# Summing the squares of the second norm: three more tiles on GpSimd, and one sum on TensorE behind the second projection

## The chip, the cores and the metric

The kernel runs on one core of one Trainium2 chip. The metric is the device time of one execution in microseconds (us), the median over several runs.

## What is computed

Two batches of 512 tokens with 1024 features go through two layers with shared weights: a pooling mixer and a SwiGLU feed-forward, then grouped-query attention (8 query heads, 2 key/value heads, head size 128, axial rotary positions) and a second SwiGLU. An RMS norm stands ahead of each of the four. The part that the change touches is the norm ahead of attention, and the projections that follow it:

```python
def rms_norm(x, g):
    xf = x.astype(jnp.float32)
    y = xf * lax.rsqrt(jnp.mean(xf * xf, axis=-1, keepdims=True) + EPS)
    return (y * g.astype(jnp.float32)).astype(x.dtype)

h = rms_norm(x, norm_mix[1])
qkv = jnp.einsum('btd,de->bte', h, w_qkv)
q, k = rms_norm(q, q_gain), rms_norm(k, k_gain)
q, k = apply_axial_rope(q, tables), apply_axial_rope(k, tables)
x = x + attention(q, k, v) @ w_o
```

## The kernel before

Each engine has its own written-out list of instructions, and semaphores tie the lists together; every engine and every DMA queue takes its list in order. The residual stream `x` lies in SBUF with features on partitions, as 8 tiles of 128 features by 512 tokens for each batch, so that a sum over features is a sum over partitions and tiles. Products with weights are made in three float32r matmuls each (high·high, high·low, low·high).

Norm k (1 to 3 in the code) works on 16 tiles in the order `SEQ[k]`; its position in that order is called `r`. ScalarE squares each tile (`square`, L1103). A squared tile goes one of two ways:

- GpSimd adds it to a running sum `stat[b]` of its batch (`add_squares`, L2422). At the end TensorE sums that one tile over partitions (`mean_square`), with four matmuls against a column of ones, one for each 128 tokens.
- Tiles in the list `DIRECT[k]` are summed by TensorE themselves (`sum_square`), four such matmuls for each tile, into the same PSUM columns.

A plain float32 matmul leaves two records in the trace, so one `mean_square` or one `sum_square` is 8 records of line L596. Then ScalarE takes the root (`root`, L1111), VectorE the reciprocal (`inverse`, L1691), TensorE spreads the result over partitions (`wide`, four transposes, L603), and ScalarE keeps it (`keep_wide`, L1117).

For norm 2, the first 12 tiles of `SEQ[2]` go through GpSimd: batch 0 wholly, and half of batch 1. The last four tiles (features 4 to 7 of batch 1) are final only when the last block of the first feed-forward, block 41, has been added to `x` (`add_rows(0, 6)`). They are in `DIRECT[2]`, and their squares lie in the four tiles `late[3:7]`. Batch 1's `mean_square(2, 1)` is placed between blocks 39 and 40 of the feed-forward's second matmul (L784).

The stretch after the feed-forward, in the order of each list:

- TensorE: `project(0)` (the first key head of batch 0, 24 matmuls, L583), `project(1)` up to feature tile 3, with `head_square(0)` (8 records, L899) after tile 1, four `sum_square` for r = 12 to 15, the rest of `project(1)` (12 matmuls), `key_wide(0)`, `wide(2, 1)`, then `values(0, ...)` in four quarters (24 matmuls each, L924) with `head_square(1)` after the first, `key_wide(1)` after the second, then `project(2)` and on. The third quarter needs weight unit 3, `key_wide(1)` needs `head_inverse(1)`.
- ScalarE: the squares r = 12 to 15, `gain(0)` (a square L1486 and a scaled copy L1487; it writes the tiles that GpSimd's running sum also reads, `tmp[4]` and `tmp[5]`, and so waits for `n_acc`), `head_root(0)`, `split(2)`, `root(2, 1)`, `gain(1)`, `keep_wide(2, 1)`, `split(3)`, `key_hi(0)`, `head_root(1)`.
- VectorE: `split_lo(1)`, `split_lo(2)`, `head_inverse(0)`, `inverse(2, 1)`, `rope(0)`, `split_lo(3)`, `key_lo(0)`, `head_inverse(1)`, `rope(1)`. `split_lo(i)` (L1684) ends the preparation of weight unit i. `rope(p)` is three instructions, L2198, L2202 and, for keys, L2206, and it waits for the rotated copy from DMA, for both rotary tables, and for GpSimd's `times_cos(p)` (L2462).
- The SP queue, which issues the DMAs: weight unit 4 (`load_att(4)`), the cosine table (L513), the sine table (L515), weight unit 5 (L383), four DMAs of 64 KB for `rotate(0)` (L503), four for `rotate(1)`, weight unit 6, and on.

The sine table is loaded into `tmp[7]`, which is also `stat[1]`, the running sum of batch 1. Its load therefore waits until `mean_square(2, 1)` has read that tile:

```python
sp.wait_ge(n_ms, 2)
sp.dma_start(sin_t[:, :], rope_sin).then_inc(tables_in, 16)
```

Of the kernel before, what the change touches and what calls it, by code (L numbers as in the profile page):

```python
# [13 lines left out]
KC = D // P  # L14
# [42 lines left out]
NBLK = (NPAIR + 1) // 2  # L57
N_BLOCK = 7 * NBLK
# [3 lines left out]
def build(nc, x_prompt, x_sample, norm_mix, norm_ffn, pool_w, pool_b, pool_scale, w_qkv, q_gain,  # L62
          k_gain, w_o, w_gu, w_down, rope_cos, rope_sin, band_tab, y_prompt, y_sample):
    with ExitStack() as ctx:
# [96 lines left out]
        b_gate, b_up, b_down = bank[0:2], bank[2:4], bank[4:8]  # L161
# [6 lines left out]
        def sem(name):  # L168
            return ctx.enter_context(nc.semaphore(name))
# [14 lines left out]
        n_sq, n_acc, n_add, n_ms, n_sqrt = sem("n_sq"), sem("n_acc"), sem("n_add"), sem("n_ms"), sem("n_sqrt")  # L184
# [52 lines left out]
        def q_of(h, b):  # L237
# [8 lines left out]
        SEQ = {1: [(c, b) for b in range(NB) for c in range(KC)],  # L246
               2: ([(c, 0) for c in range(4, 8)] + [(c, 1) for c in range(4)] + [(c, 0) for c in range(4)]
                   + [(c, 1) for c in range(4, 8)])}
# [2 lines left out]
        GAIN = {1: V_FFN, 2: V_MIX + KC, 3: V_FFN + KC}  # L251


        DIRECT = {1: SEQ[1], 2: SEQ[2][12:], 3: SEQ[3][15:]}
        ACC0, ADD0 = {1: 0, 2: 0, 3: 10}, {1: 0, 2: 16, 3: 20}

        def acc_count(k, r):

            return ACC0[k] + sum(1 for cb in SEQ[k][:r + 1] if cb[0] != HEAD[k][cb[1]] and cb not in DIRECT[k])

        def add_count(k, r):

            return ADD0[k] + sum(1 for cb in SEQ[k][:r + 1] if cb in DIRECT[k])

# [3 lines left out]
        def last_of(k, b):  # L268
            return max(i for i, cb in enumerate(SEQ[k]) if cb[1] == b and cb not in DIRECT[k])

# [88 lines left out]
        def _(sp):  # L359
# [139 lines left out]
            def rotate(p):  # L499

                sp.wait_ge(p_gain, p + 1)
                for dst, src in ((0, 1), (1, 0), (2, 3), (3, 2)):
                    sp.dma_start(rot[p % 2][32 * dst:32 * dst + 32, :],  # L503
                                 qg[p % 2][32 * src:32 * src + 32, :]).then_inc(rot_in[p % 2], 16)
# [3 lines left out]
            for i in range(NB * N_QKV):  # L508
                load_att(i + RAW)
                b, j = i // N_QKV, i % N_QKV  # L510
                if i == 1:
                    sp.wait_ge(n_lo, KC)
                    sp.dma_start(cos_t[:, :], rope_cos).then_inc(tables_in, 16)  # L513
                    sp.wait_ge(n_ms, 2)
                    sp.dma_start(sin_t[:, :], rope_sin).then_inc(tables_in, 16)  # L515
                elif i == 2:
                    for p in range(KVH):
                        rotate(p)
                elif b == 1 and j < 2:
                    rotate(N_PROJ * b + j)  # L520
                elif j >= 4:
                    rotate(N_PROJ * b + j - 2)
# [55 lines left out]
        def _(pe):  # L578
# [8 lines left out]
            def three(whi, wlo, mhi, mlo):  # L587
                return [(whi, mhi), (whi, mlo), (wlo, mhi)]
# [27 lines left out]
            def mean_square(k, b, out):  # L616

                pe.wait_ge(n_acc, acc_count(k, last_of(k, b)))
                return columns(stat[b], out, True)
# [189 lines left out]
            def swiglu(layer):  # L809
                k = 2 * layer + 1  # L810
                gate_up(layer, 0, 1)
                if layer == 0:
                    sum_square(1, 14, bank[3])
                else:
                    mean_square(3, 1, bank[3])
                sum_square(k, 15, bank[3])
                gate_up(layer, 0, 2)
                wide(k, 1, bank[5])
                gate_up(layer, 1, 1)
                gate_up(layer, 1, 2)  # L820
                gate_up(layer, 0, 5)
                gate_up(layer, 2, 1)
                gate_up(layer, 1, 5)
                gate_up(layer, 2, 2)
                gate_up(layer, 0, 6)
                gate_up(layer, 0, 3)
                gate_up(layer, 1, 6)
                gate_up(layer, 0, 7)
                gate_up(layer, 1, 3)
                gate_up(layer, 0, 4)  # L830
                gate_up(layer, 1, 7)
                gate_up(layer, 1, 4)
                gate_up(layer, 2, 6)
                gate_up(layer, 2, 5)
                gate_up(layer, 2, 7)
                gate_up(layer, 2, 3)
                gate_up(layer, 2, 4)
                for i in range(3, NF):
                    gate_up(layer, i, 1)
                    gate_up(layer, i, 5)  # L840
                    gate_up(layer, i, 6)
                    gate_up(layer, i, 3)
                    gate_up(layer, i, 7)
                    gate_up(layer, i, 2)
                    gate_up(layer, i, 4)
                for b in range(N_BLOCK):
                    if layer == 0 and b == N_BLOCK - NBLK + 2:
                        mean_square(2, 0, bank[1]).then_inc(n_ms, 1)
                    elif layer == 0 and b == N_BLOCK - NBLK + 3:
                        wide(2, 0, bank[1])  # L850
                    elif layer == 0 and b == N_BLOCK - NBLK + 4:
                        mean_square(2, 1, b_up[1]).then_inc(n_ms, 1)
                    if layer == 1 and N_BLOCK - NBLK < b < N_BLOCK - NBLK + 4:
                        u = 4 * (b - (N_BLOCK - NBLK + 1))
                        for i in range(u, u + 4):
                            turn_y(i)
                    down_block(layer, b)
# [4 lines left out]
            def project(p, out, bank_free, ks=range(KC)):  # L862

                b, u = p // N_PROJ, unit_of("p", p)
                if 0 in ks:
                    if bank_free > 0:
                        pe.wait_ge(p_gain, bank_free)
                    if p == N_PROJ:
                        pe.wait_ge(n_lo, 2 * KC)
                    elif p == N_PLAIN - 1:  # L870
                        pe.wait_ge(v_lo_done, 2)
                    elif p == N_PLAIN:
                        pe.wait_ge(v_lo_done, 4)
                    pe.wait_ge(w_lo, u + 1)
                for k in ks:
                    whi, wlo = w_chunk(u, k)
                    if p == 0:
                        pe.wait_ge(n_lo, k + 1)
                    product(out[:, :], three(whi, wlo, half_hi[b][:, k, :], half_lo[b][:, k, :]),
                            k == 0, k == KC - 1, proj_done if k == KC - 1 else None)  # L880
                    if k == 1 and p > 0 and p not in (KVH, N_PLAIN):
                        if p <= N_PLAIN:
                            head_square(p - 1, b_up[(p - 1) % 2], p - 2)
                        else:
                            head_square(p - 1, b_side[1][:, NT * (p - 1 - N_PLAIN):], N_PLAIN + 4 if p == N_PLAIN + 5 else 0)
# [44 lines left out]

            project(0, b_gate[0], 0)
            project(1, b_gate[1], 0, range(4))
            for r in range(12, 16):
                sum_square(2, r, b_up[1])
            project(1, b_gate[1], 0, range(4, KC))
            key_wide(0, b_up[0])
            wide(2, 1, b_up[1])
            values(0, b_down[0:2], 0)
# [138 lines left out]
        def _(act):  # L1077
# [7 lines left out]
            def square(k, r, ready):  # L1085

                c, b = SEQ[k][r]
                ready(c, b)
                if (c, b) in DIRECT[k]:
                    dst = sq_tile(k, r)  # L1090
# [14 lines left out]
            def root(k, b, src):  # L1105

                if k > 1 and b == 0:
                    act.wait_ge(n_ms, 2 * k - 3)
                else:
                    act.wait_ge(n_add, add_count(k, KC * (b + 1) - 1))  # L1110
                nc.scalar.activation(n_inv[:, NT * b:NT * (b + 1)], src[:, 0:NT], ACT.Sqrt, bias=epst[:, 0:1],  # L1111
                                     scale=1.0 / D).then_inc(n_sqrt, 1)
# [364 lines left out]
            def gain(p, src):  # L1477

                act.wait_ge(proj_done, p + 1)
                if p >= 2:  # L1480
                    act.wait_ge(p_done, p - 1)
                    act.wait_ge(p_ms, p - 1)
                elif p == 0:
                    act.wait_ge(n_acc, acc_count(2, 11))
                g = V_KG if p % N_PROJ < KVH else V_QG
                nc.scalar.activation(qsq[p % 2][:, :], src[:, :], ACT.Square).then_inc(p_sq, 1)  # L1486
                nc.scalar.activation(qg[p % 2][:, :], src[:, :], ACT.Copy,  # L1487
                                     scale=vec[:, g:g + 1]).then_inc(p_gain, 1)
# [96 lines left out]
            for a in range(16):  # L1585
                kind, n = BESIDE[a]
                for sc in range(4):
# [3 lines left out]
                    r = 4 * a + sc  # L1591
# [812 lines left out]
        def _(pool):  # L2404
# [8 lines left out]
            def add_squares(k, r):  # L2413

                c, b = SEQ[k][r]
                if c == HEAD[k][b] or (c, b) in DIRECT[k]:
                    return
# [137 lines left out]
```

## Time and profile before

| | |
|---|---|
| median of 3 runs | 1755.0 us (1750.07 to 1757.45) |
| the profiled execution | 1759.22 us |
| its span in the profile | 1757.0 us |
| TensorE, mean granted clock | 0.988 |
| TensorE matmuls, busy | 1720.0 us, 98% of the span |
| VectorE busy | 1153.2 us, 66% |
| ScalarE busy | 749.0 us, 43% |
| GpSimd busy | 131.9 us, 8% |

Times within the profile count from the start of the span. PE is TensorE's matmuls, PEld its weight loads, DVE VectorE, ACT ScalarE, POOL GpSimd, SPq the DMA queue of SyncE. The granted clock is given as a share of full speed: 1.00 is 2.4 GHz and 0.50 is 1.2 GHz. The end of a matmul in the records is modelled, so the start of one is the safer number.

### The profile page before, as it was taken

How to read it: one execution, taken by the hardware profiler on the slowest of the kernel's cores; microseconds unless marked ns; L12 is line 12 of the kernel's file. 1: busy time of each engine (PE TensorE's matmuls, PEld its weight loads, DVE VectorE, ACT ScalarE, POOL GpSimd, SP SyncE). 2: the span in 40 equal slices, each digit the busy share in tenths (PEclk: the TensorE clock that was granted, in tenths of full speed). 3: DMA queues.
4: the chain of work that ended last, by engine and by line, in shares of the span. 5: the costliest groups of instructions: out<-in, count | busy, mean ns of one | idle time of the engine just before them, and what ended most of it. 6: DMA issues, size and time to landing. Idle time of an engine off the chain costs nothing.

```text
span 1757.0 us, 21487 instructions
## 1 busy us (share of the span) xinstructions
PE 1720.0 (98%) x7993; PEld 1431.4 (81%) x7993; DVE 1153.2 (66%) x1636; ACT 749.0 (43%) x1149; POOL 131.9 (8%) x108
## 2 busy tenths in 40 slices
PE   7999999999999999999999999999999999999998
PEld 6877888888888888888887788778888888788887
DVE  5497566666657766556778877986656656576744
ACT  5554333333333435444556564443333333333332
POOL 1010000000000003023123312300000000000000
PEclk9799999999999999999999999999999999999999
DMA  4004333323367333333121113043433333483333
GB/s 176 13 25 151 107 96 109 102 91 107 115 221 262 90 98 97 92 101 99 55 63 51 47 48 97 24 126 97 131 97 96 117 93 96 162 326 100 96 102 114
DMA packets 185786, 188.43 MB, mean 107 GB/s; under 512 B 8354, under 2 KB 138452, under 8 KB 185684
## 3 DMA queue, kind: packets, MB, share of 16 engines
q1 hardware_dynamic: 112784, 150.34, 26.4%
q10 hardware_dynamic: 72900, 36.73, 7.3%
q8 instruction: 64, 1.05, 0.2%
q14 instruction: 38, 0.31, 0.1%
HBM read 137.23 MB, written 44.56 MB: 103 GB/s over the span
## 4 chain that ended last, share of the span: by engine, by line
PE 90%; DVE 5%; issue 1%; ACT 1%; DMA 1%; POOL 0%; SPq 0%; ACTq 0%; POOLq 0%; DVEq 0%
PE bank L759 46%; PE bank L784 24%; PE bank L583 14%; PE bank L971 2%; PE bank L596 1%; PE bank L669 1%; PE bank L924 1%; DVE raw_max L2255 1%; PE bank L899 1%; DVE aw L1684 1%; DVE nmax L2261 1%; DMA raw<-act_d 0%; DVE f_t L1732 0%; PE bank L806 0%; DVE f_t L1737 0%
## 5 line engine op out<-in xcount | busy, mean ns | idle before, releaser
L759 PE MATMUL bank<-h_T,ring 128*128 128x512 f32 x2112 | 502.6, 390 | 3.0 <-DVE tmp L1824 1.6
L759 PEld LDWEIGHTS bank<-h_T,ring 128*128 128x128 f32 x2112 | 395.4, 188 | 89.9 <-DVE h_T L1743 3.9
L784 PE MATMUL bank<-a,w 128*128 128x512 f32 x1848 | 421.1, 389 | 2.1 <-DVE a L1894 2.1
L784 PEld LDWEIGHTS bank<-a,w 128*128 128x128 f32 x1848 | 346.2, 188 | 74.6 <-issue 2.9
L759 PE MATMUL bank<-h_B,ring 128*128 128x512 f32 x1584 | 382.0, 390 | 2.9 <-DVE ring L1806 2.8
L759 PEld LDWEIGHTS bank<-h_B,ring 128*128 128x128 f32 x1584 | 296.6, 188 | 66.1 <-DVE ring L1806 3.7
L1806 DVE TENSOR_TENSOR ring<-raw,ring 128x512 fp32r<-128x512 f32 (+1 forms) x180 | 146.2, 813 | 42.6 <-ACT ring L1189 42.6
L1189 ACT CAST ring<-raw 128x512 fp32r<-128x512 f32 (+1 forms) x180 | 128.6, 717 | 84.9 <-PE bank L759 68.2
L1890 DVE TENSOR_TENSOR w<-wd_A,w 128x1024 fp32r<-128x1024 f32 x72 | 82.6, 1148 | 102.7 <-ACT w L1260 102.7
L1260 ACT CAST w<-wd_A 128x1024 fp32r<-128x1024 f32 x72 | 70.6, 981 | 179.7 <-PE bank L784 179.7
L583 PE MATMUL bank<-half_hi,aw 128*128 128x512 f32 x320 | 113.1, 406 | 0.0
L1818 DVE TENSOR_TENSOR tmp<-bank,tmp 128x512 f32<-128x512 f32 x44 | 30.4, 690 | 115.6 <-PE bank L759 115.5
L1894 DVE TENSOR_TENSOR a<-raw,a 128x1024 fp32r<-128x1024 f32 x84 | 97.0, 1155 | 12.2 <-ACT a L1262 12.2
L1262 ACT CAST a<-raw 128x1024 fp32r<-128x1024 f32 x84 | 82.1, 977 | 17.1 <-DMA raw<-act_d 17.1
L583 PE MATMUL bank<-o_hi,aw 128*128 128x512 f32 x256 | 86.7, 397 | 1.1 <-POOL o_lo L2497 1.1
L2422 POOL TENSOR_TENSOR tmp<-tmp,tmp 128x512 f32<-128x512 f32 x23 | 34.6, 1506 | 672.4 <-ACT tmp L1103 671.7
L1189 ACT CAST ring<-s_tmp 128x1024 fp32r<-128x1024 f32 (+1 forms) x46 | 46.7, 1015 | 79.9 <-PE bank L759 76.8
L1560 ACT ACTIVATE prob<-bank,nmax,q_inv 128x512 f32<-128x512 f32 x64 | 49.9, 780 | 54.3 <-DVE nmax L2261 54.2
L583 PEld LDWEIGHTS bank<-half_hi,aw 128*128 128x128 f32 x320 | 61.5, 192 | 12.6
L1225 ACT ACTIVATE tmp<-tmp 128x512 f32<-128x512 f32 x44 | 27.8, 632 | 100.1 <-DVE tmp L1824 100.1
L1806 DVE TENSOR_TENSOR ring<-s_tmp,ring 128x1024 fp32r<-128x1024 f32 (+1 forms) x46 | 54.1, 1177 | 17.4 <-ACT ring L1189 17.4
L583 PE MATMUL bank<-half_lo,aw 128*128 128x512 f32 x160 | 63.4, 396 | 0.0
(181 smaller groups left out, 2052.7 us busy)
## 6 DMA issues: line engine op xcount, KB each, us to landing
act_d<-tmp SPq DMA_DIRECT2D x154, 256.0 KB, 3.1
raw<-in_ffn_w_gate_up ACTq DMA_DIRECT2D x70, 512.0 KB, 3.9
raw<-act_d SPq DMA_DIRECT2D x70, 512.0 KB, 3.6
wd_A<-in_ffn_w_down SPq DMA_DIRECT2D x40, 512.0 KB, 8.3
raw<-in_attn_w_qkv SPq DMA_DIRECT2D x24, 512.0 KB, 3.9
raw<-in_ffn_w_gate_up SPq DMA_DIRECT2D x18, 512.0 KB, 3.9
raw<-in_attn_w_o SPq DMA_DIRECT2D x16, 512.0 KB, 3.8
tmp<-tmp SPq DMA_DIRECT2D x80, 64.0 KB, 2.0
```

Source lines behind the costliest of these rows:

```text
L583: ins = pe.matmul(out, w, m, start=first and i == 0, stop=last and i == n - 1)
L759: ins = pe.matmul(out[:, :], w, m, start=k in (1, 2, 5) and j == 0 and t == 0, stop=k in (2, 3, 4) and j == 3 and t == 2, skip_group_check ...
L784: ins = pe.matmul(banks[m][:, :], w, h, start=q in (0, 1, 3) and first and t == 0, stop=q in (1, 5, 6) and jj == NBLK - 1 and t == 2, skip ...
L971: ins = pe.transpose(b_turn[r % 3][:, i * P:(i + 1) * P], prob[:, i, sc * P:(sc + 1) * P], ident[:, :])
L1189: nc.scalar.copy(dst, src).then_inc(f_hi, 1)
L1260: nc.scalar.copy(w2[:, k % 3, 0:n, 0, :], src).then_inc(w2_hi, 1)
L1262: nc.scalar.copy(a2[:, (k + 1) % 3, 0:n, 0, :], raw2[:, act_slot(layer, k), 0:n, :]).then_inc(a2_hi, 1)
L1560: nc.scalar.activation(prob[:, i, :], b_score[s % 2][:, :], ACT.Exp, bias=nmax[:, s % 8:s % 8 + 1], scale=q_inv[:, s:s + 1], accum_out=rsu ...
L1806: nc.vector.tensor_tensor(lo, src, hi.bitcast(F32), ALU.subtract).then_inc(f_lo, 1)
L1890: nc.vector.tensor_tensor(w2[:, k % 3, 0:n, 1, :], src, w2[:, k % 3, 0:n, 0, :].bitcast(F32), ALU.subtract).then_inc(w2_lo, 1)
L1894: nc.vector.tensor_tensor(a2[:, s, 0:n, 1, :], raw2[:, act_slot(layer, k), 0:n, :], a2[:, s, 0:n, 0, :].bitcast(F32), ALU.subtract).then_i ...
L2422: nc.gpsimd.tensor_tensor(out=stat[b][:, :], in0=stat[b][:, :], in1=sqr[i % 2][:, :], op=ALU.add).then_inc(n_acc, 1)
```

## The change

Three of the last four tiles of squares (r = 12 to 14) leave `DIRECT[2]`, so that GpSimd adds them to `stat[1]`. TensorE no longer sums `stat[1]` between blocks 39 and 40, nor the four tiles in the middle of `project(1)`; it does one `mean_square(2, 1)` and one `sum_square(2, 15)` after the whole of `project(1)`. The load of the sine table now waits for the count that `sum_square(2, 15)` raises, and `gain(0)` for GpSimd's thirteenth addition in place of its tenth. Squares r = 12 to 14 are written to the pair `sqr`, and the square r = 14 waits for the addition of r = 12. The other lines adapt counts.

```diff
-        DIRECT = {1: SEQ[1], 2: SEQ[2][12:], 3: SEQ[3][15:]}
-        ACC0, ADD0 = {1: 0, 2: 0, 3: 10}, {1: 0, 2: 16, 3: 20}
+        DIRECT = {1: SEQ[1], 2: SEQ[2][15:], 3: SEQ[3][15:]}
+        ACC0, ADD0 = {1: 0, 2: 0, 3: 13}, {1: 0, 2: 16, 3: 17}
...
-                    sp.wait_ge(n_ms, 2)
+                    sp.wait_ge(n_add, add_count(2, 15))
                     sp.dma_start(sin_t[:, :], rope_sin).then_inc(tables_in, 16)
...
-                    elif layer == 0 and b == N_BLOCK - NBLK + 4:
-                        mean_square(2, 1, b_up[1]).then_inc(n_ms, 1)
...
             project(0, b_gate[0], 0)
             project(1, b_gate[1], 0, range(4))
-            for r in range(12, 16):
+            project(1, b_gate[1], 0, range(4, KC))
+            mean_square(2, 1, b_up[1])
+            for r in range(15, 16):
                 sum_square(2, r, b_up[1])
-            project(1, b_gate[1], 0, range(4, KC))
             key_wide(0, b_up[0])
             wide(2, 1, b_up[1])
...
-                    act.wait_ge(n_ms, 2 * k - 3)
+                    act.wait_ge(n_ms, k - 1)
...
-                    act.wait_ge(n_acc, acc_count(2, 11))
+                    act.wait_ge(n_acc, acc_count(2, 14))
```

## Rows read from the trace of the kernel before

**Rows 1.** The page: its first line, and the chain that ended last, by engine.
```profile
span 1757.0 us, 21487 instructions
...
PE 90%; DVE 5%; issue 1%; ACT 1%; DMA 1%; POOL 0%; SPq 0%; ACTq 0%; POOLq 0%; DVEq 0%
```

**Rows 2.** The chain in order of time: start us, us, what.
```profile
725.02 6.80 PE bank L583 x30
731.82 0.79 PE bank L899 x8
...
734.11 4.56 PE bank L596 x32
738.66 4.97 PE bank L583 x12
...
744.51 2.88 PE bank L924 x24
...
751.15 0.44 PE bank L603 x4
```

**Rows 3.** Stretches of half a us: PE busy (instructions), granted clock, DMA share, GB/s.
```profile
736.00:736.50 0.50, 0.50 (x6) 0.75 0.35 103
...
743.00:743.50 0.50, 0.50 (x4) 0.92 0.00 0
```

**Rows 4.** The timeline of TensorE in norms 1 and 3: start us, us, instruction, what it waited for.
```profile
68.83 1.95 PE L596 MATMUL bank<-ones,tmp 128*128 128x1 f32 x16 [0.59 <-ACT tmp L1103]
...
1108.91 1.84 PE L596 MATMUL bank<-ones,tmp 128*128 128x1 f32 x16
```

**Rows 5.** Stretches of one us there, columns as in rows 3.
```profile
70.00:71.00 1.00, 1.00 (x9) 0.83 0.00 0
...
1110.00:1111.00 1.00, 1.00 (x9) 1.00 0.21 61
```

**Rows 6.** The timeline of ScalarE.
```profile
725.31 2.42 ACT L1103 ACTIVATE late<-x 128x512 f32<-128x512 f32 x4 [0.40 <-DVE x L1933]
730.49 0.60 ACT L1486 ACTIVATE tmp<-bank 128x512 f32<-128x512 f32 x1 [2.76 <-PE bank L583]
...
738.70 0.26 ACT L1111 ACTIVATE n_inv<-bank,epst 128x4 f32<-128x4 f32 x1 [4.86 <-PE bank L596]
```

**Rows 7.** GpSimd's additions of squares: duration ns min/median/max.
```profile
L2422 POOL TENSOR_TENSOR tmp<-tmp,tmp x23: 1274/1296/2100, 671.4 to 1103.1; 128x512 f32<-128x512 f32 x23
```

**Rows 8.** The timeline of GpSimd.
```profile
695.33 8.00 POOL L2422 TENSOR_TENSOR tmp<-tmp,tmp 128x512 f32<-128x512 f32 x4 [4.74 <-ACT tmp L1103]
740.17 1.71 POOL L2462 TENSOR_TENSOR tmp<-tmp,tmp 128x512 f32<-128x512 f32 x1 [36.84 <-DMA tmp<-tmp]
```

**Rows 9.** The timeline of VectorE.
```profile
697.63 2.31 DVE L1894 TENSOR_TENSOR a<-raw,a 128x1024 fp32r<-128x1024 f32 x1
...
726.99 1.21 DVE L1684 TENSOR_TENSOR aw<-raw,aw 128x1024 fp32r<-128x1024 f32 x1
...
739.00 0.18 DVE L1691 RECIPROCAL n_inv<-n_inv 128x4 f32<-128x4 f32 x1 [3.81 <-ACT n_inv L1111]
740.06 0.69 DVE L2198 TENSOR_TENSOR tmp<-tmp,tmp 128x512 f32<-128x512 f32 x1 [0.88 <-DMA tmp<-tmp]
741.92 0.69 DVE L2202 TENSOR_TENSOR tmp<-tmp,tmp 128x512 f32<-128x512 f32 x1 [1.16 <-POOL tmp L2462]
...
746.30 1.22 DVE L1684 TENSOR_TENSOR aw<-raw,aw 128x1024 fp32r<-128x1024 f32 x1 [1.44 <-ACT aw L1083]
747.44 0.68 DVE L2213 TENSOR_TENSOR k_lo<-tmp,k_hi 128x512 fp32r<-128x512 f32 x1
```

**Rows 10.** The timeline of the SP queue: DMA issues.
```profile
735.12 0.38 SPq L383 DMA_DIRECT2D raw<-in_attn_w_qkv  x1
...
744.87 2.42 SPq L503 DMA_DIRECT2D tmp<-tmp  x4
```

**Rows 11.** DMA issues from 725 to 760 us: count, KB each, median us to landing.
```profile
tmp<-tmp SPq DMA_DIRECT2D x8, 64.0 KB, 2.3
```

## The prediction

> **What bounds the kernel now.** The page comes first: TensorE carries 90% of the chain that ended last, so time on its list counts, and time elsewhere only where TensorE waits for it [rows 1]. The chain in order of time, read from 715 to 757 us, then shows that TensorE alone is on it through the whole stretch of the change: the matmuls of `project(0)` and the first six of `project(1)` up to 731.82, `head_square(0)`, the four `sum_square` from 734.11 for 4.56 us, the last 12 matmuls of `project(1)` for 4.97 us, the values from 744.51 and `key_wide(1)` at 751.15 [rows 2]. One of these terms is too long. 30 matmuls of the same shape took 6.80 us, 0.227 each; the 12 took 4.97, 0.414 each [rows 2]. The windows give the reason: the granted clock left 1.00 in the half us from 736.0 and was back in the one from 743.0 [rows 3], so it was at 1.2 GHz for some 6.8 us, after 2.1 us of `sum_square`. That dip is the dearest thing here. At full clock 32 records would be four times the 0.79 of `head_square(0)`, 3.2 us, and the 12 matmuls 2.72, so the dip cost 1.4 + 2.25 = 3.6 us.
>
> Everything below is summed against the profiled execution: span 1757.0, its time 1759.22, which lies 4.2 above the median of 1755.0 that the forecast is given for.
>
> **The change, part by part.**
>
> *The sum between blocks 39 and 40 goes.* It is 8 records of L596, priced as `head_square(0)`, 0.79 us [rows 2]. TensorE then comes to `project(0)` 0.79 earlier. Whether it keeps that is decided by the next part.
>
> *GpSimd adds three tiles more.* The four squares run from 725.31, 0.6 each [rows 6], and follow VectorE's additions to `x`, which end the same as before. So the first GpSimd addition starts at about 725.95. An addition takes 1.30 in the median and 2.10 at most [rows 7]; four beside VectorE's big two-input subtractions took 8.00, and one of these took 2.31 where its like took 1.21 alone [rows 8, 9]. GpSimd and VectorE hold each other up in such pairs. `split_lo(1)` at 726.99 is such a subtraction and must fall among the three. Three additions and one subtraction in turn give 725.95 + 3 × 1.30 + 1.21 = 731.05. Bounds: 729.85 with no collision, 732.25 at 2.10 each. `gain(0)` now waits for the third, and starts at 731.05 in place of 730.49 [rows 6]; its square ends 0.6 later, 731.65, and `head_square(0)` waits for that. Before, the square ended at 731.09 and TensorE's modelled end of the matmuls ahead is 731.82; matmuls overlap, so I take a start 0.3 late, bounds 0.8 early and 1.2 late. The 0.79 of the part above is thus spent waiting at `head_square(0)`. `split_lo(1)` may end 1.3 late, which `project(1)` at about 729.5 hardly feels, and behind `head_square(0)` it is nothing. The square r = 14 waits for one addition, 0.7 us, while ScalarE has nothing else before `gain(0)`.
>
> The Trainium skill (SBUF — State Buffer, "SBUF: two separate sides") says that VectorE and GpSimd share one port pair under an exclusive lock, held for a whole instruction. Row and rule agree on the collision, and by the rule exactly one collision is due here, which is the value taken.
>
> *On TensorE the columns shrink and move.* `project(1)` runs through: 12 × 0.227 = 2.72 from 734.4 to 737.15. Then 16 records where there were 32. Sixteen took between 2 × 0.79 and 1.84 [rows 2, 4], so 1.7, to 738.85. `key_wide(0)` takes 0.44 [rows 2], to 739.3. `wide(2, 1)` now has no projection to hide its chain: the root 0.26, the reciprocal 0.18 and three hand-overs of 0.05 (738.70 + 0.26 to 739.00 is 0.04) [rows 6, 9] make 0.6 after the columns, 739.45; `key_wide(0)` covers all but 0.15. With the spread of 0.44 the values start at about 740.0, against 744.51 [rows 2]: 4.5 us early. That is 1.5 from the removed columns at full clock (2.86 with the clock), 2.25 from the projection at full clock, less 0.3 and 0.15.
>
> *The sine table is loaded late.* This is the part that speaks against the change. Its issue waited for nothing before. Now it waits for the last column, 738.85, and behind it in the SP queue stand weight unit 5, `rotate(0)` and `rotate(1)`. One large issue takes 0.38 [rows 10], so table and weights take 0.8 and `rotate(0)` begins at 739.7, where it began right behind the weights, at 735.5, before. Four small issues take 2.42 together, so the last starts 1.8 after the first, and lands 2.3 after that [rows 10, 11]: 743.8. Before, 4.5 lay between 735.5 and `rope(0)` at 740.06 [rows 9], which would make it 744.2; I take 744.1. So `rope(0)` starts 4.0 later than before.
>
> Behind it on VectorE stand `split_lo(3)`, `key_lo(0)` and `head_inverse(1)`, and TensorE waits for the first (third quarter of the values) and the last (`key_wide(1)`). The times: GpSimd's `times_cos(0)` 1.71 with its hand-overs puts L2202 1.86 after the start of L2198 (740.06, 741.92), and 0.69 for it and 0.69 for L2206 (the same shape, and no longer held by `key_wide(0)`) end `rope(0)` 3.3 after its start, 747.4. `split_lo(3)` 1.22, `key_lo(0)` 0.68, a reciprocal 0.18 and hand-overs 0.1: 749.6 [rows 8, 9]. `times_cos(1)` is due just then and can hold `split_lo(3)` up, by nothing or by up to 1.7; I add 0.3. `key_wide(1)` at 749.9.
>
> TensorE comes to `key_wide(1)` 751.15 − 744.51 = 6.64 after the start of the values [rows 2], at 746.65, and waits 3.25 us. Of the 4.5 us gained, 751.15 − 749.9 = 1.25 is left. What comes after is dense matmuls that need nothing of this chain, so it stays.
>
> *The clock.* Nearest rows: 16 records alone in norm 3 left the clock at 1.00; 16 behind a wait of 0.59 in norm 1 were followed by a fall to 0.50 within the stretch after them [rows 4, 5]. The new run of columns, spread, wait and spread is some 2.9 us without one large matmul, longer than that, so a fall at about 740 is likelier than none. It would stretch the values by no more than 12 matmuls' worth, 2.25 us, and these lie ahead of the wait of 3.25: nothing is lost, and the wait is only shorter. The second place is that wait. If the clock falls there, up to 2.25 come on the path. With the first fall the wait is about 1 to 1.5 us and a second is unlikely; without it, likely. The price here is 0, bounds 0 and 2.25.
>
> The Trainium skill (TensorE: Matmul & The Clock Gate, "Part 4: PE-mode transpose") says that transposes do not count as TensorE activity for its clock. No row separates that. By it the two spreads are empty time, which makes the first fall likelier and changes no term.
>
> *Sum:* −0.79 + 0.79 (wait at `head_square(0)`) + 0.3 − 1.5 − 1.4 − 2.25 + 0.15 + 3.25 = −1.45, with roundings between −1.25 and −1.45. I take −1.3: the profiled execution would become 1758, the median 1753.7.
>
> **The rivals.**
>
> 1. *The rotary chain is hidden after all.* If `rope(0)`, `split_lo(3)` and `head_inverse(1)` end before TensorE arrives, all 4.5 us are kept: 1750.5. For it: nothing but quicker landings, and even at 2.0 us less the wait is over 1. It needs two hand-overs of the SP queue to be cheaper than shown. 8 in 100.
> 2. *Slower: the clock falls in the wait at `key_wide(1)`.* Place: behind the values' second quarter; price: up to 2.25; it decides once it costs more than the 1.3 left. Then +1, 1756. If `times_cos(1)` holds `split_lo(3)` for a whole 1.7 as well, 1757.5. For it: the rows of norm 1. Against it: a first fall shortens the wait. 27 in 100.
> 3. *GpSimd is late.* The change then moves the wait ahead instead of removing work. At 2.10 for each addition the whole chain is 0.9 later than summed: −0.4, 1754.6. 10 in 100.
> 4. My forecast, 1753.7, with its own range of 1752.5 to 1754.8 for the mechanism alone: 55 in 100.
>
> **How the numbers follow.** All four cases lie between 1750.5 and 1757.5, within 0.3% of the median. About 0.5%, 8.8 us, is what a measurement of this kernel can tell from no change; the three runs shown spread over 7.4 us for one and the same kernel. So the range is the cases' 1750.5 to 1757.5, widened by that spread's part on a median: 1749.5 to 1759. For more than 0.5% either way the change would have to give its whole 4.5 us twice over, or a chain of the attention stage would have to break; 2 in 100 faster, 2 slower, 96 the same.
>
> **What the profile after would show.** TensorE: the 12 matmuls of `project(1)` at 0.23 each right behind the six before, and 16 records of L596 behind them, done near 739. Wrong if the clock is below 1.00 there. SP queue: the sine table's issue right after these, near 739, and L503 from about 739.7. VectorE: L2198 first near 744, late by 4. TensorE: a wait of 1 to 3 us ahead of the second L603 of `k_inv`, put down to VectorE's reciprocal L2185. GpSimd: three L2422 between 726 and 731, and a short wait of TensorE or ScalarE for the last. Granted clock: a dip from about 740, over by 744; a dip from 748 or later would be rival 2. The prediction fails if `key_wide(1)` finds its input ready (rival 1), or if the stages after 757 us do not simply move with it.

## The result, and the profile after

| | before | after |
|---|---|---|
| first timing, median | 1755.4 us (1750.07 to 1760.18, 17 runs) | 1761.26 us (1755.39 to 1769.2, 17 runs) |
| ratio, 95% interval | | 1.0031 (1.0019 to 1.0042) |
| second timing, median | 1755.77 us (21 runs) | 1760.74 us (10 runs) |
| ratio, 95% interval | | 1.0023 (1.0003 to 1.0042) |
| the first profiled execution | 1759.22 us | 1755.39 us |

The change makes the kernel slower, by 0.2 to 0.3%. The prediction said 1753.7 us, inside 1749.5 to 1759.0. It missed the sign and the range; that the difference stays within 0.5% held.

The profiled execution of the changed kernel is *shorter* than that of the kernel before. That is a trap, and the profile shows it: it was the fastest of the changed kernel's 17 executions. The page of the changed kernel:

```profile
span 1753.2 us, 21445 instructions
```

Both kernels are the same up to the first `mean_square(2, 0)`. Before it stood at 703.56 in the chain, here at 697.38: the 6.2 us were won ahead of the change, by fewer stretches at the low clock, mostly in norm 1 (the last section has the sums). So times of the two profiles must be compared from a common mark. The measure is the stage from `mean_square(2, 0)` to the first matmul of `project(2)`, called the stage below. By the chain it ends at 751.15 + 0.44 + 5.75, 757.33, before, and at 754.28 after: 53.8 us against 56.9. The stage became 3.1 longer.

The chain of the changed kernel, in order of time (start us, us, what), the lines that answer to [rows 2]:

```profile
697.38 0.87 PE bank L596 x8
...
725.59 1.05 PE bank L897 x8
726.64 4.21 PE bank L583 x18
730.86 1.69 PE bank L596 x16
...
735.33 4.11 DMA tmp<-tmp
...
739.58 1.72 POOL tmp L2461
741.30 0.02 issue
741.32 1.75 DVE tmp L2201
743.07 0.02 issue
743.09 0.69 DVE tmp L2205
743.77 0.89 DVE aw L1683
...
745.65 1.12 PE bank L603 x4
746.77 7.51 PE bank L922 x48
754.28 6.83 PE bank L583 x30
```

The first half went as worked out. Just ahead of 725.59 this chain runs over GpSimd's third addition and `gain(0)`, since TensorE now waits for them. The 18 matmuls of `project(1)` took 4.21, at 0.23 each, and the 16 columns 1.69. Then the chain leaves TensorE, which [rows 2] never did: it goes to the rotation's DMA, GpSimd, VectorE and back to TensorE at `key_wide(1)`. The last two TensorE lines are slow: 1.12 for a spread that took 0.44, and 7.51 for 48 matmuls that took 5.75 before.

What TensorE waited for from 715 to 760 us (total, times, longest):

```profile
PEld bank L603 <- DVE k_inv L2184: 5.5, 1, 5.5
PE bank L603 <- DVE k_inv L2184: 5.3, 1, 5.3
...
PE bank L897 <- ACT tmp L1485: 0.9, 1, 0.9
```

A wait of 5.3 us at `key_wide(1)`, and one of 0.9 at `head_square(0)`. The granted clock around them, in stretches of one us (PE busy, clock, DMA share, GB/s):

```profile
732.00:733.00 1.00, 1.00 (x9) 1.00 0.00 0
733.00:734.00 1.00, 0.92 (x9) 1.00 0.42 68
...
742.00:743.00 1.00, 0.00 (x0) 1.00 0.00 0
743.00:744.00 1.00, 0.00 (x0) 0.92 0.00 0
...
749.00:750.00 1.00, 1.00 (x7) 0.50 0.02 5
750.00:751.00 1.00, 1.00 (x7) 0.66 0.73 217
```

The values start at 733.51, in the second of these rows; TensorE's timeline has

```profile
733.51 0.48 PE L922 MATMUL bank<-aw,half_hi 128*128 128x256 f32 x2
```

The clock stayed at 2.4 GHz through columns, spreads and the wait between them, and fell to 1.2 GHz inside the long wait, for 6.8 us. The SP queue, which answers to [rows 10]:

```profile
722.71 0.58 SPq L513 DMA_DIRECT2D tmp<-in_rope_cos  x1
732.57 0.34 SPq L515 DMA_DIRECT2D tmp<-in_rope_sin  x1
732.95 0.43 SPq L383 DMA_DIRECT2D raw<-in_attn_w_qkv  x1
733.43 6.11 SPq L503 DMA_DIRECT2D tmp<-tmp  x8
```

The sine table stands 9.3 us behind the cosine table, right behind the last column, and weights and rotations follow it. GpSimd's timeline, answering to [rows 8] (VectorE's, below, to [rows 9]):

```profile
719.89 4.96 POOL L2421 TENSOR_TENSOR tmp<-tmp,tmp 128x512 f32<-128x512 f32 x3 [22.74 <-ACT tmp L1102]
739.58 2.93 POOL L2461 TENSOR_TENSOR tmp<-tmp,tmp 128x512 f32<-128x512 f32 x2 [14.73 <-DMA tmp<-tmp]
```

VectorE's first two instructions of `rope(0)`:

```profile
739.47 0.69 DVE L2197 TENSOR_TENSOR tmp<-tmp,tmp 128x512 f32<-128x512 f32 x1 [6.42 <-DMA tmp<-tmp]
741.32 1.73 DVE L2201 TENSOR_TENSOR tmp<-tmp,tmp 128x512 f32<-128x512 f32 x1 [1.16 <-POOL tmp L2461]
```

GpSimd's three additions took 4.96 us, against 5.1 worked out. The second `times_cos` now falls on `rope(0)` and stretches its addition from 0.69 to 1.73.

### The profile page after: what moved, and what is told of

The parts are those of the page before. It is cut to its first block, busy times and chain, and to the rows that moved or that the text cites. A ratio compares the mean times of both kernels' runs of the same rounds, so it can differ in the third digit from the quotient of the medians.

```text
span 1753.2 us, 21445 instructions
## 1 busy us (share of the span) xinstructions
PE 1709.5 (98%) x7969; PEld 1421.6 (81%) x7969; DVE 1157.0 (66%) x1636; ACT 748.9 (43%) x1149; POOL 136.2 (8%) x111
## 4 chain that ended last, share of the span: by engine, by line
PE 88%; DVE 7%; ACT 2%; issue 1%; DMA 1%; POOL 0%; SPq 0%; ACTq 0%; DVEq 0%; POOLq 0%
PE bank L759 45%; PE bank L784 23%; PE bank L583 14%; PE bank L970 2%; PE bank L596 1%; PE bank L897 1%; PE bank L669 1%; DVE raw_max L2254 1%; DVE aw L1683 1%; PE bank L922 1%; DVE f_t L1731 1%; DVE nmax L2260 1%; DMA raw<-act_d 0%; PE bank L806 0%; DVE ring L1805 0%
## 5 line engine op out<-in xcount | busy, mean ns | idle before, releaser
L2421 POOL TENSOR_TENSOR tmp<-tmp,tmp 128x512 f32<-128x512 f32 x26 | 39.4, 1515 | 695.4 <-ACT tmp L1102 694.4
```

The source lines that it names most:

```text
L2421: nc.gpsimd.tensor_tensor(out=stat[b][:, :], in0=stat[b][:, :], in1=sqr[i % 2][:, :], op=ALU.add).then_inc(n_acc, 1)
```

## The experiments

Three theories. **A**: the late sine table and what is queued behind it make TensorE wait at `key_wide(1)`, and its clock falls in the wait. **B**: GpSimd's three additions are the loss, through the wait at `head_square(0)`. **C**: what hurts is that root, reciprocal and spread lost the projection that hid them.

Experiments 1 to 7 and 9 were timed 12 times each, beside 21 to 35 runs of the kernel before on the same chip; the groups ran on different chips, so rows are best compared by their ratios. The stage length is read from one profile of each, as above, from `mean_square(2, 0)` in the chain to the first matmul of `project(2)`; the changed kernel has three profiles (the first, experiments 8 and 10), the kernel before two.

| kernel | median us | ratio to before (95%) | wait at `key_wide(1)` | stage us |
|---|---|---|---|---|
| before | 1755.4 to 1757.5 | | 0 | 53.8, 53.8 |
| changed | 1761.3, 1760.7 | 1.0031 (1.0019, 1.0042), 1.0023 (1.0003, 1.0042) | 5.3, 5.1, 5.4 | 56.9, 56.8, 57.3 |
| changed, sine early | 1753.9 | 0.9982 (0.9969, 0.9995) | 0 | 50.8 |
| changed, columns midway | 1756.6 | 0.9998 (0.9988, 1.0008) | 1.5 | 50.7 |
| both | 1753.1 | 0.9972 (0.9957, 0.9986) | 0.5 | 49.6 |
| both, no wait for GpSimd | 1750.4 | 0.9970 (0.9956, 0.9984) | 0 | 47.8 |
| before, sine late | 1755.6 | 0.9997 (0.9984, 1.0010) | 0.7 | 54.7 |
| changed, rotations first | 1757.7 | 1.0008 (0.9993, 1.0023) | 3.1 | 54.0 |
| changed, no GpSimd share | 1763.5 | 1.0034 (1.0017, 1.0052) | 4.5 | 58.4 |
| changed, wait filled | 1761.2 | 1.0026 (1.0010, 1.0042) | 0.8 (rest filled) | 54.7 |

**1. The sine table early.** Batch 1's running sum moves to a tile that this change left unused, so nothing holds back the sine table.

```diff
+        stat2 = [stat[0], late[6]]
...
-        sq_ring = {1: [tmp[4], tmp[5], tmp[2], tmp[1]], 2: late[3:7], 3: [tmp[2]]}
+        sq_ring = {1: [tmp[4], tmp[5], tmp[2], tmp[1]], 2: late[3:6], 3: [tmp[2]]}
...
-                    sp.wait_ge(n_add, add_count(2, 15))
                     sp.dma_start(sin_t[:, :], rope_sin).then_inc(tables_in, 16)
```
(and `stat2[b] if k == 2 else stat[b]` where norm 2 squares into, adds to and sums that tile)

> The changed kernel, but norm 2 keeps batch 1's running sum in a tile of its own, so the sine table is loaded right behind the cosine table. Theory A (the late sine table, and the rotations behind it, make TensorE wait 5.3 us ahead of key_wide(1) and let its clock fall): the wait shrinks to under 0.5 us, no clock of 1.2 GHz lies behind it, and the time is 4 to 9 us below the changed kernel, so 1752 to 1757 beside 1761.3. Theory B (the loss comes from GpSimd's three additions, which hold up gain(0) and the head's squares): the time stays within 2 us of the changed kernel.

Measured: 1753.87 us, a median 7.4 under the changed kernel's in its own group, and 0.18% under the kernel before on the same chip. The wait at `key_wide(1)` is gone, that at `head_square(0)` is still 0.9. The chain of this kernel:

```profile
727.44 5.85 PE bank L583 x18
...
742.83 0.44 PE bank L603 x4
743.27 5.75 PE bank L922 x48
```

Theory A holds, B falls: GpSimd's work and its wait are unchanged here. Theory C falls as well, since root, reciprocal and spread stand behind the projection here too. No low clock lies at `key_wide(1)`, as expected, but a stretch at 1.2 GHz did show elsewhere, behind the 0.9 us wait and the 8 records of `head_square(0)`, on the matmuls of `project(1)`:

```profile
727.00:728.00 1.00, 1.00 (x7) 1.00 0.48 174
728.00:729.00 1.00, 1.00 (x5) 0.74 0.00 0
```

**2. The columns midway.** The two sums go back into the middle of `project(1)`; the sine table still waits.

```diff
             project(1, b_gate[1], 0, range(4))
+            mean_square(2, 1, b_up[1])
+            sum_square(2, 15, b_up[1])
             project(1, b_gate[1], 0, range(4, KC))
-            mean_square(2, 1, b_up[1])
-            sum_square(2, 15, b_up[1])
```

> The changed kernel, but its mean_square and sum_square stand in the middle of project(1), where the sums stood before; the sine table still waits for them. Theory A: its load starts 2.7 us earlier, while the values start the same, so the wait ahead of key_wide(1) falls from 5.3 to about 2.5 us; time 1757 to 1759. Theory C (what hurts is that root, reciprocal and spread have no projection to hide them): the wait at wide(2, 1) was 0.3 us in the changed profile, so by that theory next to nothing, under 1 us, is won.

Measured: 1756.64, level with the kernel before and just under the expected range. The wait fell further than expected, to 1.5, and the clock did not fall in it:

```profile
PE bank L603 <- DVE k_inv L2184: 1.5, 1, 1.5
PE bank L897 <- ACT tmp L1485: 0.9, 1, 0.9
```

So the placement behind the projection was costly, but, with experiment 1, not for the reason of theory C: it started the sine table 2.8 us later (35.19 after the mark, here 32.43). Another 1.3 came from the rotations: `rope(0)` started 4.7 after their first issue here (736.50 to 741.24) and 6.0 in the changed kernel (733.43 to 739.47).

The time does not follow the stage here. This stage is 3.1 shorter than that of the kernel before, and the time by its ratio only 0.4 less (from 2.1 less to 1.4 more). One profile cannot say whether other executions had a longer stage or lost the time elsewhere.

**3. Both.**

> Both: running sum in its own tile with the sine table early, and the columns in the middle of project(1). Theory A: no wait of TensorE over 0.5 us between project(1) and project(2), and 16 columns fewer than before: 1751 to 1755, the fastest of all, 1 to 4 us under the kernel before. Theory B: no better than the changed kernel, 1759 to 1762.

Measured: 1753.14, ratio 0.9972. It did beat the kernel before. Its interval overlaps that of the first experiment; only the stage, 49.6 against 50.8, sets the two apart, and that is the low clock at 728 of the first (5.85 us for 18 matmuls that took 4.21 in the changed kernel), less the 0.5 that this one waits at `key_wide(1)`.

**4. The kernel before with its sine table late.** The wait alone.

```diff
-                    sp.wait_ge(n_ms, 2)
+                    sp.wait_ge(n_add, add_count(2, 15))
```

> The kernel before, with one edit: the sine table's load waits for the last of the four sum_square. Theory A: the rotary chain starts some 7 us after the last column here too, so key_wide(1) is about as late as in the changed kernel while the values start up to 4.5 us later than there; TensorE waits 1 to 4 us at key_wide(1): 1757 to 1760. Theory B: GpSimd adds nothing more here, so the time stays that of the kernel before, within 1 us.

Measured: 1755.62, ratio 0.9997; a wait of 0.7, and a stage 0.9 longer. Theory A's size was wrong here, its mechanism not. `key_wide(1)` came 48.3 us after the mark (748.90 − 700.60), as late as in the changed kernel (745.65 − 697.38), which was expected. But the late table costs next to nothing while TensorE is itself late, with 32 column records and a low clock in front of the values. The wait became dear only when the same change brought TensorE 4.8 us earlier to the values: 744.51 − 703.56 = 40.95 after the mark in the kernel before, 733.51 − 697.38 = 36.13 in the changed one.

**5. No wait for GpSimd.** Experiment 3, and the squares r = 12 to 14 in tiles of their own, so that `gain(0)` may overwrite the old pair.

```diff
+        sqr2 = late[4:6]
...
-                    dst = sqr[i % 2]
+                    dst = (sqr2 if k == 2 and r >= 12 else sqr)[i % 2]
...
-                    act.wait_ge(n_acc, acc_count(2, 14))
+                    act.wait_ge(n_acc, acc_count(2, 11))
```

> The kernel with both edits (running sum in its own tile with the sine table early, columns in the middle of project(1)), and the squares that GpSimd adds last in a pair of tiles of their own, so that gain(0) no longer waits for GpSimd's thirteenth addition. Three profiles show TensorE waiting 0.9 us at head_square(0). If that wait is on the path, it goes, and the time is 0.5 to 1 us under that of the kernel with both edits; if TensorE then only waits later, the two are equal.

Measured: 1750.43, ratio 0.9970, which does not part it from experiment 3 (another chip, overlapping intervals). In the profile TensorE never waits in the stage, which is 1.8 shorter than in experiment 3:

```profile
725.59 0.79 PE bank L898 x8
726.37 1.51 PE bank L584 x6
727.88 1.68 PE bank L597 x16
729.56 2.83 PE bank L584 x12
732.39 0.87 PE bank L604 x8
733.27 2.87 PE bank L923 x24
```

This is the shortest stage of all, 6.0 under the kernel before.

**6. The rotations first.** The changed kernel, with the rotations ahead of weight unit 5 on the SP queue.

```diff
                     sp.dma_start(sin_t[:, :], rope_sin).then_inc(tables_in, 16)
-                elif i == 2:
-                    for p in range(KVH):
-                        rotate(p)
+                    rotate(0)
+                    rotate(1)
```

> The changed kernel, but on the SP queue rotate(0) and rotate(1) go ahead of weight unit 5. In the changed profile the rotation's last DMA took 4.1 us to land, beside 2.3 in the median before, with 768 KB of table and weights issued just ahead. If these 512 KB of weights are what is ahead of it, rope(0) starts 1.5 to 2.5 us sooner after the last column, the wait at key_wide(1) falls from 5.3 to 3 to 4 us, and the time by as much or more, to 1758 to 1760. If the table alone sets the landing, under 0.5 us is won.

Measured: 1757.69, ratio 1.0008; wait 3.1. The DMA to landing of L503 in this kernel (min/median/max us):

```profile
DMA to landing us min/median/max: 1.9/2.1/2.9
```

The longest landing fell from 4.1 to 2.9. From the reciprocal of `inverse(2, 1)` to `rope(0)` it was 4.96 us (737.22 to 742.18) where the changed kernel took 6.60 (732.87 to 739.47), 1.6 less; another 0.6 went behind it, where `times_cos(1)` no longer fell on the addition of `rope(0)`. So 2.2 of the 5.3 us went with the order of the queue. Of the 1.6, 0.5 is the issue of the weights itself (the first rotation was issued 0.08 behind the reciprocal, 0.56 in the changed kernel). The rest is the landing of `rotate(0)`'s fourth DMA, 4.1 us in the changed kernel and 2.9 here. That the 512 KB of weights made it 4.1 is not shown: in experiment 2 they stood ahead just the same, and the fourth landed in 2.8. Its first three landed in 3.9, 3.5 and 3.1 there, in 4.1, 3.7 and 3.2 in the changed kernel, and in 2.1 to 2.4 without the weights ahead. What held the fourth up stays open.

**7. No share for GpSimd.** The changed placement, with `DIRECT[2] = SEQ[2][12:]` and `range(12, 16)` as before, so 40 records stand behind `project(1)`.

> The placement of the changed kernel, but GpSimd adds no more than before: one mean_square and four sum_square (40 records in place of 16) stand behind the whole of project(1). Theory A: the wait at key_wide(1) keeps its 5 us, since values and sine table move back alike; on top come 24 records at 0.10, 2.4 us, with a clock that falls, less the 0.9 at head_square(0): 2 to 5 us above the changed kernel, 1763 to 1766. Theory B (GpSimd's additions are the loss): below the changed kernel.

Measured: 1763.49, ratio 1.0034, which the timing cannot tell from the changed kernel's 1.0031. The stage is 1.5 longer, the wait 4.5. The clock fell behind the 40 records, from 744.4 on for 3.4 us, and once more at `key_wide(1)`. Theory B would have this kernel faster than the changed one, and neither its ratio nor its stage is; that GpSimd's share is a gain rests on the one stage alone.

**8. The changed kernel once more.**

> The changed kernel once more, for its profile. If the clock's fall in the wait at key_wide(1) belongs to the change, it is at 1.2 GHz behind that wait here too, for 3 to 7 us, and the wait is 5 us or more; if it was chance, the clock stays at 2.4 GHz.

Measured: one execution, of 1758.60; a wait of 5.1, again 6.8 us at 1.2 GHz, the same two slow lines in the chain:

```profile
748.97 1.12 PE bank L603 x4
750.09 7.53 PE bank L922 x48
```

**9. The wait filled.** 20 matmuls on operands at hand, into an idle bank.

```diff
             values(0, b_down[0:2], 1)
+            for i in range(20):
+                pe.matmul(bank[7][:, :], half_hi[0][:, i % KC, 0:P], half_hi[0][:, 0, :], start=True, stop=True)
             key_wide(1, b_side[0])
```

> The changed kernel, with 20 matmuls of 128x512 added on TensorE between the values' second quarter and key_wide(1), into a bank that nobody reads; they take 4.5 us of the wait of 5.2. It parts the wait from the clock. Theory A with the clock: key_wide(1) starts as late as before, but the clock stays at 2.4 GHz, key_wide(1) takes 0.44 in place of 1.12 and the values' second half 5.75 in place of 7.5; the stage from mean_square(2, 0) to project(2) falls from 56.8 to 54.4 us and the time by 2 to 2.5. If the clock fell for another reason than the empty wait, nothing changes.

Measured: `key_wide(1)` comes 48.3 us after the mark (752.10 − 703.76), as in the changed kernel (745.65 − 697.38), but the clock stays up:

```profile
752.10 0.65 PE bank L603 x4
752.75 5.75 PE bank L922 x48
```

The stage is 54.7, 2.2 shorter than in the changed kernel. This parts the loss: 2.2 us of the stage are the clock's price, and the length of the wait is untouched by it. The timing does not show this gain: 1.0026, beside 1.0023 for the changed kernel in the same group, with intervals too wide to tell 2 us. It is 1.8 to 7.4 us above the kernel before, where the stage is only 0.9 longer; in this execution the time outside the stage was longer too.

**10 and 11. Both kernels anew.**

> The changed kernel, timed anew beside the kernel before. The stage from mean_square(2, 0) to project(2) is 3.1 us longer than before in two profiles, while the first timing gave 5.5 us more (3.3 to 7.4). If the stage is all of it, the ratio comes out near 1.0018; if something else is slower too, near 1.0031 again. The profile: wait of 5.1 to 5.3 us, stage 56.8.

> The kernel before once more, for its profile. If its clock falls in the four sum_square every time, the stage from mean_square(2, 0) to project(2) is 53.8 us again, with a stretch at 1.2 GHz of 3 to 7 us; if that was chance, the stage is near 50.2 us, and the change cost up to 6.6.

Measured: 1760.74 against 1755.77, ratio 1.0023, whose interval holds both 1.0018 and 1.0031, so it does not decide. The stage of the changed kernel was 57.3. That of the kernel before was 53.8 again, and its clock fell in the four `sum_square` again, for 6.8 us, here in the chain of its second profile:

```profile
734.18 4.40 PE bank L596 x32
738.59 5.12 PE bank L583 x12
```

## Why the prediction was wrong, step by step

- *The sum between blocks 39 and 40, and GpSimd's three additions*: right. The additions took 4.96 us for 5.1, with the one collision taken, and the 0.79 us turned into a wait of 0.9 at `head_square(0)`.
- *Columns and projection on TensorE*: right. The values began 36.1 us after the mark; the forecast's 740.0 is 36.4.
- *The sine table is loaded late*: the right chain, its size too small. The wait at `key_wide(1)` was taken as 3.25 and measured 5.1 to 5.4. Laid over the profile before (6.18 later), `rope(0)` started at 745.65 where 744.1 was forecast, and `key_wide(1)` at 751.83 where 749.9 was. The landing made 1.55 of it: for the last DMA of `rotate(0)` 2.3 was taken, with 0.3 added by hand, and it took 4.1. The 2.3 was a median over eight DMAs; the four of `rotate(0)` in the same trace took 3.4, 3.1, 2.7 and 2.6. The rest, 0.4, is the collision: `times_cos(1)` held `rope(0)`'s addition up by 1.0 (0.69 to 1.73), against an allowance of 0.3 and hand-overs taken too long.
- *The clock*: the wrong place. A fall was expected in the run of columns and spreads, where it would have been hidden; in none of the three profiles of the changed kernel did it fall there. It fell in the wait each time, at 2.4 on the path (0.68 on `key_wide(1)`, 1.76 on the values) where 0 was taken. Of this, 0.2 is not the clock's: the spread took 0.65 behind a wait in experiments 2, 4 and 9 at full clock, against 0.44 with none. That leaves the 2.2 of experiment 9. The prediction's own sign for it, a dip from 748 or later, is in the profile: 743.84 is 750.0 laid over the profile before. Rival 2 was this, priced at up to 2.25 and given 27 in 100; it was worth more than the 1.3 that the forecast had left.
- Together: −1.3 + 2.0 + 2.4 = +3.1, which is what the stage shows (56.9 − 53.8). In the stage, the prediction's failure is these two terms.
- *The range*: its slowest case added the clock to the collision, but no case added a longer landing of the rotations, though the landing was the one term read from a queue that the change itself made fuller. Both timings lie above its end, at 1761.3 and 1760.7.
- *Still open*: the first timing gave 5.5 us (3.3 to 7.4), the stage explains 3.1, just under that interval. The second timing allows 3.1. In experiments 2 and 9 as well the time lies above what the stage would give. Whether some 2 us more are lost elsewhere is not settled, nor how much the stage differs between executions. From `project(2)` to the end of the span it is 998.9, 998.8 and 1002.4 us in the changed kernel's profiles, and 999.7 and 999.4 before, so no profile shows a place behind the stage that is regularly longer.

The Trainium skill (TensorE: Matmul & The Clock Gate, "Part 4: PE-mode transpose") says that the full clock does not engage for transposes, which do not count as busy in the same way. Two spreads and 16 columns in a row, with a short wait, left it at 1.00 in every profile of the changed kernel, so no run here shows harm from them; the empty wait of 5 us lowered it in all three.

## What to carry to other kernels

When two buffers share a tile, moving the last read of one moves the first load of the other, and everything queued behind that load. Before moving work later, ask which DMA waits for its count, and what stands behind it on that queue; here a tile that the change itself had freed removed the whole loss, and turned 0.2 to 0.3% slower into 0.2% faster (0.3% with the sums back in the projection, which the timing does not part from it). A wait is dearer than its length where it lets the clock fall, so a wait and the clock's price behind it belong in one bound, added and not weighed as alternatives.

## What the runs showed that was not expected

- The same kernel's executions differ by several us through the clock alone, far from any change. Summing 2 × (1 − clock) over stretches of one us ahead of 690 us gives 27.3 and 23.9 us at 1.2 GHz in two profiles of the kernel before, and 13.6, 20.5 and 10.2 in three of the changed kernel, in code that is the same. This is why a single profile, with a span of 1753.2, looked faster while the kernel is slower.
- A wait of 0.9 us followed by 8 column records was followed by a fall in one profile (the first experiment), and left the clock alone in the others with the same wait. At `key_wide(1)`, waits of 0.5 to 1.5 us brought no fall in four profiles (in one of them with the 20 matmuls of experiment 9 ahead), and empty waits of 3.1 to 5.4 us brought one in all five.
